# A hybrid decoder layer on one core: the middle stage rewritten as one schedule by weight chunk

## The chip, the core and the metric

One core of a Trainium2 chip runs the whole kernel. TensorE (PE) multiplies and writes to PSUM (eight banks of 512 columns), VectorE (DVE) and ScalarE (ACT) work between PSUM and SBUF, GpSimd (POOL) on SBUF alone, and SyncE (SP) issues most DMAs. Each engine runs its own instructions in order, and they wait for one another on semaphores. The metric is the device time of an execution in microseconds; lower is better.

## The reference

256 prompt tokens of one sequence and one new token for each of 8 decoding sequences (264 columns, N) go through one layer, in fp32:

```
x = LN(a*x + 0.5*(silu(x Wg) * (x Wu)) Wd)          # D 2048, F 5632
z = x W_in -> q, k, v (8 heads, 2 maps of 64) | b, c, h (1024 each) | gate_attn, gate_conv (2048 each)
q, k = rope(q), rope(k)
o = (softmax(q1 k1) - lam * softmax(q2 k2)) v        # prompt: causal over 256
                                                     # samples: 8 pages of 128 cached keys/values each, and the new token
y_attn = (headnorm(o) * g * 0.8) W_attn_out
y_conv = (b * conv3(c * h)) W_conv_out
x = LN(a*x + (sigmoid(gate_attn)*y_attn + sigmoid(gate_conv)*y_conv) W_o)
x = LN(a*x + 0.5*(silu(x Wg2) * (x Wu2)) Wd2)
```

Outputs are x, the new keys and values, and the last convolution inputs. `page_table` says which 128-row page of `cache_k` and `cache_v` each of a sequence's 8 pages is.

## The kernel before

**Chunks and products.** Activations lie with features on partitions and the 264 tokens in the free dimension. Every fp32 operand is split in a high and a low part that TensorE takes in a fast fp32 form (F32R), and a product of 128 x 128 weights is three matmuls (`products`, L512 to L514: x_hi w_hi, x_lo w_hi, x_hi w_lo). Weights come in chunks of 512 KB, 256 rows by 512 columns: SP loads one into a slot of `w_raw` (a ring of 4, `chunk`, L356), ACT copies it rounded to `w_hi` (`split_hi`, L845), DVE subtracts to get `w_lo` (`split_lo`, L1144), and PE runs 24 matmuls. The load of chunk n waits for the split of chunk n - 4, ACT's split waits for PE to have used chunk n - 4. ACT and DVE are written three chunks ahead of PE (LEAD). A panel is the sum over chunks for 512 output columns (four PSUM banks, one for each 128 columns): 8 chunks for `w_in`, 4 for the two inner projections. In most places two sets of four banks alternate.

**The stages.** First feed-forward block and norm; queries (two panels side by side, 16 chunks); keys (16); values (16); b, c, h (48 chunks, all on banks 0 to 3); three of four pairs of gate panels in a loop (48); two panels of the conv output (8); then the last gate pair (16) and the last two conv panels (8) with the value pages between their chunks; then the attention output, `W_o`, norm, second feed-forward block and norm.

**Keys of the samples.** The sample queries are stored to memory and broadcast to all partitions (`q_bcast`, all eight sequences, L482 and L485, on POOL's queue). A page of keys is loaded into one of two or four slots (`k_page`, L388), multiplied on POOL (L495), and summed by head on DVE (L1349). 16 pages go with the value panels, one page a chunk; the other 48 with every second chunk up to the last gate loop.

**Prompt attention.** It stands between the chunks of b, c, h, one head every five chunks (`at_head`): scores of both maps (L690, L691; map 0 on partitions 0 to 63, map 1 on 64 to 127; banks 4 and 5), mask and maximum on DVE, exp on ACT, weights on DVE (L1446, L1449), three transposes (L699), values (L708 to L710). The head norm squares two heads at a time on ACT, sums over partitions with a matmul of ones on 512 columns (L742, L812), takes roots and scales on DVE (L1474, L1476).

**Values of the samples.** A page goes through the weight ring: it is loaded into `w_raw`, split by ACT and DVE like a weight chunk, and multiplied by the page's weights, high and low in 16 columns (`page_values`, L783: four matmuls of 512 columns to 16 partitions). After 8 pages ACT copies the sums out and `turn_seq` turns them with one-column matmuls (L798), at every second sequence with the new token's values (L794). At the end come the samples' norm (L825) and the split of o into `o_hi` and `o_lo` (L1109, L1601), for which the first products of the attention output wait.

Of the kernel before, what the change touches and what calls it, by code (L numbers as in the profile page):

```python
# [8 lines left out]

# [6 lines left out]
ALU = mybir.AluOpType  # L16
ACT = mybir.ActivationFunctionType
F32 = mybir.dt.float32
# [4 lines left out]
P = 128  # L23
# [24 lines left out]
PT = 2  # L48

# [50 lines left out]
def program(nc, a, out):  # L100
    with ExitStack() as ctx:
# [38 lines left out]
        page_ids = at("page_ids", [1, B * PAGES], I32)  # L140
# [21 lines left out]
        o_all = at("o_all", [P, HEADS, N])  # L162
        scores = at("scores", [P, B, SLOTS, 2 * HEADS])
        k_ring = at("k_ring", [P, 2, DC])
        qb_at = (top + 31) // 32 * 32
        q_bcast = at("q_bcast", [P, B, DC])
        m_hi = at("m_hi", [P, DT, N], F32R, qb_at)
        m_lo = at("m_lo", [P, DT, N], F32R, qb_at + DT * TILE)
        v_s = at("v_s", [B, DC])
        assert 2 * DT * TILE <= (B + 1) * DC * 4  # L170
        early = (top + 31) // 32 * 32

        z_q = at("z_q", [P, AT, N])
        z_k = at("z_k", [P, AT, N])
        v_tok = at("v_tok", [P, PT, DC])
        z_v = at("z_v", [P, AT, N])

        zv_at = early + 2 * AT * TILE + PT * DC * 4
# [4 lines left out]
        top = early  # L183
        sig = at("sig", [P, 2, DT, N])
        assert zv_at + AT * TILE <= top

        c_at = top
# [3 lines left out]
        qk_tok = at("qk_tok", [P, 3, DC], F32, c_at + AT * TILE)  # L191

        k_slots = [k_ring[:, 0], k_ring[:, 1], qk_tok[:, 0], qk_tok[:, 1]]
        stats = at("stats", [P, 16])
        s_tmp = at("s_tmp", [B, 2, 2 * HEADS])

        u = z_c[:, 2]
        conv_o = z_c[:, 1]
        conv_t = at("conv_t", [P, 3, AT, B], F32, ln_at)
        conv_new = at("conv_new", [P, AT, B, 2], F32, ln_at + 768)  # L200
        o_sqp = at("o_sqp", [P, 2, T], F32, ln_at + 1280)
        yc_hi = at("yc_hi", [P, AT, N], F32R, c_at)
        yc_lo = at("yc_lo", [P, AT, N], F32R, c_at + 2 * AT * TILE)
        o_hi = at("o_hi", [P, AT, N], F32R, c_at)
        o_lo = at("o_lo", [P, AT, N], F32R, c_at + AT * TILE)

        kr_at = qb_at - 2 * DC * 4
        s_max = at("s_max", [P, P], F32, kr_at)
        s_diag = at("s_diag", [P, P], F32, kr_at + 512)
        s_rec = at("s_rec", [P, P], F32, kr_at + 1024)  # L210
        s_attn = at("s_attn", [P, B, SLOTS, HEADS], F32, kr_at + 1536)
        s_attn2 = at("s_attn2", [P, B, SLOTS, HEADS], F32, kr_at + 4096)
        s_col = at("s_col", [P, 1], F32, kr_at + 7168)

        s_weights = at("s_weights", [P, B, PAGES, 2, HEADS], F32R, qb_at)
        s_sums = at("s_sums", [2 * HEADS, DC], F32, qb_at + 4096)
        o_sqs = at("o_sqs", [P, HEADS * B], F32, qb_at + 8192 + 32)
        own_head = at("own_head", [2 * HEADS, HEADS], F32, qb_at + 8192)
# [41 lines left out]
        new_scored = sem("new_scored")  # L260
        q_stored = sem("q_stored")
        qb_landed = sem("qb_landed")
        k_landed = [sem(f"k_landed{i}") for i in range(4)]
        k_mult = sem("k_mult")
        k_free = sem("k_free")
        sc_done = sem("sc_done")
# [7 lines left out]
        o_ready = sem("o_ready")  # L274
        conv_done = sem("conv_done")
# [11 lines left out]
        ss_rec = sem("ss_rec")  # L287
        ss_attn = sem("ss_attn")
        pv_weights_hi = sem("pv_weights_hi")
        pv_weights = sem("pv_weights")  # L290
        seq_out = sem("seq_out")
        seq_turned = sem("seq_turned")
        seqs_out = sem("seqs_out")
        o_square = sem("o_square")
        o_normed = sem("o_normed")
        o_sumsq = sem("o_sumsq")
        o_std = sem("o_std")
# [18 lines left out]
        CONSTS, MADE = 16 * 7, 8  # L316
# [3 lines left out]
        V_TURN, K_BACK, FIRST_HEAD, HEAD_CH = 1, 5, 7, 5  # L320
# [6 lines left out]
        TURN_EVEN = {K_CH: 3, A_CH: 2}  # L327

        def through_page(chunks, k):

            c = next(c for c in range(chunks) if sum(PAGES_AFTER[chunks][:c + 1]) >= k)
            return c + 1 + k

        def sums_bank(b):

            return 4 * (1 - b // 2 % 2) + (2 if b % 2 == 0 else 0)

        HEAD_NORM = 3

        def at_head(h):  # L340
            return FIRST_HEAD + HEAD_CH * h

        assert at_head(HEADS) <= 2 * C_PAIRS * K_CH - 1
        assert KC * WC == DC and 2 * len(VALUE_PANELS) == B


        @block.sync
        def _(sp):
            n = Count()
            pages = Count()  # L350
# [30 lines left out]
            def page_numbers(seq):  # L381

                return nc.values_load_multi_w_load_instructions(
                    page_ids[0:1, bass.ds(seq * PAGES, PAGES)], engines=[mybir.EngineType.SP],
                    min_val=0, max_val=a["cache_k"].shape[1] - 1)[1]

            def page(cache, p, dst):
                return sp.dma_start(dst, cache[0, bass.ds(p, 1)].rearrange("a k h e -> (a k) (h e)"))  # L388

            def w_in_panel(i, p, after=None):  # L390
                for c in range(K_CH):
                    chunk(a["w_in"][0], KC * c, i * (2 * WC) + p * WC)
                    if after is not None:
                        after(c)

            def k_page(seq_ids, j, slot, free):
                sp.wait_ge(k_free, free)
                page(a["cache_k"], seq_ids[j], k_slots[slot]).then_inc(k_landed[slot], 16)

            def w_in_pair(i, seq):  # L400

                ids = page_numbers(seq)
                for p in range(2):
                    def keys(c):
                        if c % 2 == 1:
                            j = (p * K_CH + c) // 2
                            k_page(ids, j, j % 2, pages.add())
                    w_in_panel(i, p, keys)
# [5 lines left out]
            for p in range(2):  # L414
                w_in_panel(1, p)

            sp.wait_ge(page_ids_in, 16)
            sp.wait_ge(back, 1)
            seq_ids = []

            def keys(c):
                if c == 0:
                    return
                for j in (c - 1,) if c < 2 * K_CH - 1 else (c - 1, c):
                    if j % PAGES == 0:
                        seq_ids[:] = page_numbers(j // PAGES)
                    pages.add()
                    k_page(seq_ids, j % PAGES, j % 4, max(j - 1, 1))
            for p in range(2):
                w_in_panel(2, p, lambda c: keys(p * K_CH + c))  # L430
            with loop(sp, B - 2, (n, 2 * K_CH), (pages, PAGES)) as i:
                w_in_pair(i + 3, i + 2)

            def v_page(number):
                sp.wait_ge(w_lo_ready, n.add())
                s = (n.n - 1) % RING
                page(a["cache_v"], number, w_raw[:, s].rearrange("p k n -> p (k n)")).then_inc(w_landed[s], 16)

            out_pair(a["w_conv_out"][0], A_CH, 0)
            for p, chunks in enumerate(VALUE_PANELS):  # L440
                ids = []
                for c in range(chunks):
                    if chunks == K_CH:
                        chunk(a["w_in"][0], KC * c, (2 + C_PAIRS + G_PAIRS) * (2 * WC) + p * WC)
                    else:
                        chunk(a["w_conv_out"][0], KC * c, 2 * WC + (p - 2) * WC)
                    done = sum(PAGES_AFTER[chunks][:c])
                    for k in range(done, done + PAGES_AFTER[chunks][c]):
                        if k % PAGES == 0:
                            ids = page_numbers(2 * p + k // PAGES)  # L450
                        v_page(ids[k % PAGES])
# [13 lines left out]
        def _(pool):  # L465
# [5 lines left out]
            pool.wait_ge(made, 5)  # L471
# [5 lines left out]
            pool.dma_start(page_ids[:], a["page_table"]).then_inc(page_ids_in, 16)  # L477
# [5 lines left out]
            pool.wait_ge(q_stored, 16)  # L483
            for b in range(B):
                pool.dma_start(q_bcast[:, b], q_scratch[b:b + 1].broadcast_to([P, DC])).then_inc(qb_landed, 16)  # L485
            pool.wait_ge(qb_landed, 16 * B)

            for page in range(B * PAGES):
                if page < 2 * PAGES:
                    slot, uses = page % 4, page // 4 + 1  # L490
                else:
                    slot, uses = page % 2, 2 * PAGES // 4 + (page - 2 * PAGES) // 2 + 1
# [11 lines left out]
        def _(pe):  # L504
# [151 lines left out]
            for j in (2, 0, 1):  # L656
                to_tokens(z_q, j)
# [1015 lines left out]
```

## Time and profile before

| | |
|---|---|
| median of 3 runs | 2441.69 us (2439.89 to 2444.42) |
| profiled execution | 2443.84 us, span 2442.0 us |
| PE busy | 2363.0 us (97%), 18783 instructions |
| DVE busy | 1449.6 us (59%) |
| ACT busy | 1051.6 us (43%) |
| POOL busy | 192.6 us (8%) |
| HBM | 467.88 MB read, 193 GB/s over the span |

"Busy" of PE is a union of overlapping matmuls whose ends are modelled; the distance from one start to the next is what a matmul costs in a row of them. A row such as `L512 ... x2` in a timeline joins neighbouring records; a plain fp32 matmul has two records, a transpose or an F32R matmul one. The clock column is the granted share of 2.4 GHz, averaged over the stretch; in any moment it is 1.2 or 2.4 GHz.

### The profile page before, as it was taken

To read this page: it belongs to the slowest core of one execution; us is meant where nothing else is said; L and a number is where in the kernel's file an instruction comes from. 1 tells how busy PE (TensorE), PEld (TensorE's weight loads), DVE (VectorE), ACT (ScalarE), POOL (GpSimd) and SP (SyncE) were. 2 spreads that over 40 slices of the span, in tenths; PEclk is the share of its full clock that TensorE was granted. 3 is DMA by queue.
4 is the path that set the end of the run, shared out by engine and by line. 5 is a ranking of instruction groups with operands and counts; after the bars stand their busy time and mean duration, and the time that the engine had idled before them with its cause. 6 is when DMAs were issued, how large, how long until landed. Compare 5 with 4: busy or idle time off the path is not lost.

```text
span 2442.0 us, 46756 instructions
## 1 busy us (share of the span) xinstructions
PE 2363.0 (97%) x18783; PEld 2300.0 (94%) x18783; DVE 1449.6 (59%) x1494; ACT 1051.6 (43%) x1230; POOL 192.6 (8%) x98
## 2 busy tenths in 40 slices
PE   8999999999999999999899998999999999999997
PEld 8999999999998998888898767999999999999997
DVE  5444544545555768888887666777445444445554
ACT  4443444443333444444445554435444344444333
POOL 1000000000000036332340000000000000000001
PEclk9999999999999999999999998999999999999998
DMA  7655555555655587665676776555555555655553
GB/s 229 189 180 181 180 171 188 178 179 179 179 176 157 163 314 254 239 220 182 221 279 208 260 249 197 190 164 169 177 182 176 184 180 173 188 180 176 180 181 114
DMA packets 230518, 474.05 MB, mean 194 GB/s; under 512 B 16792, under 2 KB 18904, under 8 KB 230400
## 3 DMA queue, kind: packets, MB, share of 16 engines
q1 hardware_dynamic: 226304, 465.76, 59.4%
q0 software_dynamic: 1440, 4.38, 0.5%
q10 hardware_dynamic: 2656, 2.24, 0.3%
q8 instruction: 86, 1.41, 0.2%
q14 instruction: 32, 0.26, 0.0%
HBM read 467.88 MB, written 4.43 MB: 193 GB/s over the span
## 4 chain that ended last, share of the span: by engine, by line
PE 83%; DVE 9%; DMA 3%; ACT 3%; issue 2%; SPq 0%; DVEq 0%; ACTq 0%
PE ps L512 27%; PE ps L513 27%; PE ps L514 26%; DVE w_lo L1144 4%; DMA w_raw<-in_w_in 2%; ACT w_hi L845 1%; DVE scores L1349 1%; PE ps L783 1%; DMA w_raw<-in_cache_v 1%; PE ps L798 1%; DVE attn L1449 1%; DVE z_c L1500 0%; DVE o_sqp L1474 0%; DMA w_raw<-in_w_conv_out 0%; ACT prob L992 0%
## 5 line engine op out<-in xcount | busy, mean ns | idle before, releaser
L1144 DVE TENSOR_TENSOR w_lo<-w_raw,w_hi 128x1024 fp32r<-128x1024 f32 x816 | 1032.5, 1275 | 871.6 <-ACT w_hi L845 868.7
L845 ACT ACTIVATE w_hi<-w_raw 128x1024 fp32r<-128x1024 f32 x816 | 858.6, 1058 | 1087.4 <-PE ps L514 891.3
L512 PE MATMUL ps<-x_hi,w_hi 128*128 128x264 f32 x4096 | 1178.0, 288 | 37.8 <-DVE w_lo L1144 16.9
L513 PE MATMUL ps<-x_lo,w_hi 128*128 128x264 f32 x4096 | 1171.5, 286 | 0.0
L514 PE MATMUL ps<-x_hi,w_lo 128*128 128x264 f32 x4096 | 1170.5, 286 | 0.0
L512 PEld LDWEIGHTS ps<-x_hi,w_hi 128*128 128x128 f32 x4096 | 779.8, 190 | 51.0 <-DVE w_lo L1144 26.6
L513 PEld LDWEIGHTS ps<-x_lo,w_hi 128*128 128x128 f32 x4096 | 778.4, 190 | 1.0 <-issue 0.7
L514 PEld LDWEIGHTS ps<-x_hi,w_lo 128*128 128x128 f32 x4096 | 776.6, 190 | 0.0
L512 PE MATMUL ps<-h_hi,w_hi 128*128 128x264 f32 x1408 | 401.3, 285 | 0.0
L513 PE MATMUL ps<-h_lo,w_hi 128*128 128x264 f32 x1408 | 400.6, 285 | 0.0
L514 PE MATMUL ps<-h_hi,w_lo 128*128 128x264 f32 x1408 | 400.2, 284 | 0.0
L514 PEld LDWEIGHTS ps<-h_hi,w_lo 128*128 128x128 f32 x1408 | 265.3, 188 | 0.0
L513 PEld LDWEIGHTS ps<-h_lo,w_hi 128*128 128x128 f32 x1408 | 265.3, 188 | 0.1
L512 PEld LDWEIGHTS ps<-h_hi,w_hi 128*128 128x128 f32 x1408 | 264.5, 188 | 0.1
L495 POOL TENSOR_TENSOR k_ring<-k_ring,q_bcast 128x1024 f32<-128x1024 f32 x56 | 149.7, 2674 | 250.4 <-DMA k_ring<-in_cache_k 250.2
L499 POOL TENSOR_TENSOR y<-y,mean 128x528 f32<-128x528 f32 x5 | 6.3, 1300 | 1146.0 <-DVE mean L1281 1146.0
L512 PE MATMUL ps<-m_hi,w_hi 128*128 128x264 f32 x256 | 73.0, 285 | 0.0
L513 PE MATMUL ps<-m_lo,w_hi 128*128 128x264 f32 x256 | 72.8, 284 | 0.0
L514 PE MATMUL ps<-m_hi,w_lo 128*128 128x264 f32 x256 | 72.7, 284 | 0.0
L1349 DVE TENSOR_REDUCE scores<-k_ring 128x16 f32<-128x1024 f32 (+1 forms) x56 | 67.7, 1210 | 0.4
L482 POOL DMA_DIRECT2D q_scratch<-q_s x1 | 0.5, 531 | 841.5 <-DVE q_s L1394 841.5
L855 ACT ACTIVATE hid<-ps 128x264 f32<-128x264 f32 x88 | 34.2, 392 | 75.5 <-PE ps L514 75.5
(217 smaller groups left out, 1362.3 us busy)
## 6 DMA issues: line engine op xcount, KB each, us to landing
w_raw<-in_ffn_w_gate SPq DMA_DIRECT2D x176, 512.0 KB, 3.5
w_raw<-in_ffn_w_up SPq DMA_DIRECT2D x176, 512.0 KB, 4.3
w_raw<-in_ffn_w_down SPq DMA_DIRECT2D x176, 512.0 KB, 3.6
w_raw<-in_w_in SPq DMA_DIRECT2D x160, 512.0 KB, 5.0
w_raw<-in_cache_v SPq DMA_DIRECT2D x64, 512.0 KB, 4.5
k_ring<-in_cache_k SPq DMA_DIRECT2D x56, 512.0 KB, 3.9
w_raw<-in_w_o SPq DMA_DIRECT2D x32, 512.0 KB, 4.1
w_raw<-in_w_conv_out SPq DMA_DIRECT2D x16, 512.0 KB, 4.8
```

The source lines that it names most:

```text
L495: nc.gpsimd.tensor_tensor(keys, keys, q_bcast[:, page // PAGES], ALU.mult).then_inc(k_mult, 1)
L499: nc.gpsimd.tensor_tensor(two, two, mean[:].rearrange("p (a n) -> p a n", a=1).broadcast_to([P, KC, N]), ALU.subtract).then_inc(ln_centred, 1)
L512: nc.tensor.matmul(acc, wh, hi[:, kt], start=(kt == 0), stop=False)
L513: nc.tensor.matmul(acc, wh, lo[:, kt], start=False, stop=False)
L514: return nc.tensor.matmul(acc, wl, hi[:, kt], start=False, stop=last)
L783: mm = nc.tensor.matmul(ps[0:2 * HEADS, bank + c], s_weights[:, b, j].rearrange("p c h -> p (c h)"), w[:, s, c], start=(j == 0 and w is w_ ...
L798: mm = nc.tensor.matmul(by_head(b)[:, 0, h:h + 1], s_sums[:, h * VD:(h + 1) * VD], own_head[:, h:h + 1], start=False, stop=True, skip_grou ...
L845: nc.scalar.activation(w_hi[:, s], w_raw[:, s], ACT.Copy).then_inc(w_hi_ready, 1)
L855: nc.scalar.activation(dst(m), ps[:, 4 * banks + m, 0:N], func).then_inc(out_of[banks], 1)
L1144: V.tensor_tensor(w_lo[:, s], w_raw[:, s], w_hi[:, s].bitcast(F32), ALU.subtract).then_inc(w_lo_ready, 1)
L1349: V.tensor_reduce(dst, keys.rearrange("p (g d) -> p g d", d=HD), AX, ALU.add).then_inc(k_free, 1)
L1449: ins = V.scalar_tensor_tensor(attn[:, b].rearrange("p b k -> p (b k)"), prob[:, 1, b].rearrange("p b k -> p (b k)"), stats[:, 14 + j:15 + j],
```

## The change

Everything from the keys' panels to the last chunk before the attention output is written as one list of 160 chunks, x = 0 to 159, without loops. Each engine goes through the list, and constants say at which x each piece of other work stands (on DVE and ACT mostly x + 3 or more, because they run ahead).

- The order of panels: keys 2, values 2, b c h 6, conv gates 4, conv output 4, attention gates 4. All are summed in banks 0 to 3; banks 4 to 7 belong to the other work.
- One ring of nine page slots (`kv_ring`) holds key pages, then value pages. Key page j is summed at chunk 8 + 27 j // 25 (chunks 8 to 76). `q_bcast` holds four sequences; POOL issues the others' broadcasts between its multiplications.
- Value pages are no longer split. At 16 steps, every four chunks from 88 to 148, one page of each of four sequences is multiplied in plain fp32: 32 weight columns for each sequence, written to partitions 0, 32, 64 and 96, in two halves of 512 columns.
- The sums of four sequences are turned at once with the constant `pick`, the new token's share comes from DVE (`v_new`, `o_new`), and `v_sample` is stored transposed.
- Prompt attention: heads start at the chunks in HEAD; the values come with tokens on partitions, so that the head norm works per partition (square sums on ACT, root, scale), in groups of 3, 2 and 3 heads, which are turned back by transposes (`turn_out`). The weights are not scaled by the first map's sum before the product.
- The turns of q, k, v, the softmax of the samples, the convolution and the samples' norm are cut in pieces that stand at chunks of the list.

```diff
-        VALUE_PANELS = [K_CH, K_CH, A_CH, A_CH]
-        PAGES_AFTER = {K_CH: (3, 3, 2, 2, 2, 2, 2, 0), A_CH: (6, 5, 5, 0)}
+        for name, w, col, count, chunks in (
+                ("k", "w_in", DC, 2, K_CH), ("v", "w_in", 2 * DC, 2, K_CH), ("c", "w_in", 3 * DC, 6, K_CH),
+                ("conv_gate", "w_in", 6 * DC + D, 4, K_CH), ("conv_out", "w_conv_out", 0, 4, A_CH),
+                ("attn_gate", "w_in", 6 * DC, 4, K_CH)):
+            for i in range(count):
+                PANELS.append((name, i, w, col + i * WC, chunks))
+        Q_TURN, K_TURN, V_TURN, LAMBDA_SUM = 0, 2 * K_CH, 4 * K_CH, 8
+        K_SUM = [8 + 27 * j // 25 for j in range(B * PAGES)]
+        K_LOAD = [j - 2 * K_CH // 2 if j < PAGE_SLOTS else K_SUM[j] - 4 for j in range(B * PAGES)]
+        SOFTMAX = K_SUM[-1] + 1
+        NEW_TOKEN = SOFTMAX + 10
+        V_STEP = [SOFTMAX + 11 + 4 * s for s in range(2 * PAGES)]
+        V_LOAD = [K_SUM[B * PAGES - PAGE_SLOTS + v] + 5 if v < PAGE_SLOTS else V_STEP[v // SEQS] + v % SEQS - 1
+                  for v in range(B * PAGES)]
+        BY_HEAD = V_STEP[PAGES - 1] + 5, V_STEP[-1] + 3
+        HEAD = 40, 52, 64, 90, 100, 117, 127, 137
+        TURN, VALUES = 6, 8
+        NORMED = (0, 1, 2), (3, 4), (5, 6, 7)
+        CONV = 84
...
+            # PE
+            def page_values(step):
+                seqs, j = step // PAGES * SEQS, step % PAGES
+                for k in range(SEQS):
+                    i = B * PAGES + SEQS * step + k
+                    pe.wait_ge(kv_landed[i % PAGE_SLOTS], 16 * (i // PAGE_SLOTS + 1))
+                for half in range(2):
+                    for k in range(SEQS):
+                        at_page = ((seqs + k) * SLOTS + j) * HEADS
+                        rows = slice(k * P // SEQS, (k + 1) * P // SEQS)
+                        mm = nc.tensor.matmul(ps[rows, 6 + half], s_flat[:, at_page:at_page + P // SEQS],
+                                              kv_ring[:, (B * PAGES + SEQS * step + k) % PAGE_SLOTS,
+                                                      half * WC:(half + 1) * WC],
+                                              start=(j == 0), stop=(j == PAGES - 1), skip_group_check=True)
+                mm.then_inc(v_free, 1)
...
+            x = 0
+            for name, i, _, _, chunks in PANELS:
+                if name == "conv_out" and i == 0:
+                    pe.wait_ge(yc_ready, 2)
+                hi, lo = (yc_hi, yc_lo) if name == "conv_out" else (x_hi, x_lo)
+                for c in range(chunks):
+                    panel_chunk(0, hi, lo, c, chunks)
+                    middle(x)
+                    x += 1
...
+            # DVE
+            for x in range(LEAD, MIDDLE + LEAD):
                 split_lo(1)
+                if x - LEAD + 1 in ends:
+                    out_of_panel(*PANELS[ends.index(x - LEAD + 1)][:2])
+                for j in range(B * PAGES):
+                    if x == K_SUM[j]:
+                        page_scores(j)
+                for h in head_at(x, 4):
+                    prompt_max(h)
+                for h in head_at(x, 7):
+                    prompt_attn(h)
...
```

## Rows read from the trace of the kernel before

**Rows 1.** The page: its head, and from part 5 the split on DVE.
```profile
span 2442.0 us, 46756 instructions
...
L1144 DVE TENSOR_TENSOR w_lo<-w_raw,w_hi 128x1024 fp32r<-128x1024 f32 x816 | 1032.5, 1275 | 871.6 <-ACT w_hi L845 868.7
```

**Rows 2.** Table of stretches: from:to, length, busy time (instructions) by engine, clock, DMA.
```profile
core 0: us, PE busy (x) PEld busy (x) DVE busy (x) ACT busy (x) POOL busy (x), PEclk, DMA share, GB/s
300.00:400.00 100.00, 100.00 (x825) 100.00 (x824) 46.94 (x44) 41.36 (x45) 0.00 (x0) 1.00 0.58 180
790.20:839.80 49.60, 48.99 (x385) 48.84 (x386) 37.84 (x53) 25.06 (x38) 0.00 (x0) 0.95 0.55 170
839.80:1498.70 658.90, 614.59 (x4546) 554.67 (x4546) 509.48 (x510) 319.75 (x425) 180.06 (x73) 0.97 0.70 240
891.00:943.00 52.00, 49.94 (x389) 47.59 (x387) 51.93 (x33) 19.12 (x25) 43.95 (x14) 1.00 0.74 265
...
1498.70:1548.20 49.50, 49.50 (x385) 49.50 (x386) 32.55 (x39) 18.31 (x20) 0.00 (x0) 0.94 0.47 145
```

**Rows 3.** Timeline of PE (start us, us, records xN): one head; the queries' transposes.
```profile
839.78 2.78 PE L636 MATMUL ps<-ident,z_q 128*8 128x128 f32 x24 [0.57 <-ACT z_q L855]
...
1035.37 0.38 PE L708 MATMUL ps<-attn_t,v_tok 128*128 128x128 f32 x2
...
1036.13 0.50 PE L690 MATMUL ps<-z_k,z_q 64*128 64x128 f32 x4
1036.46 0.61 PE L691 MATMUL ps<-z_k,z_q 64*128 64x256 f32 x4
1036.99 0.39 PE L512 MATMUL ps<-x_hi,w_hi 128*128 128x264 f32 x1
```

**Rows 4.** Timeline of PE: turning a sequence's sums; value pages at both clocks.
```profile
1333.47 1.94 PE L794 MATMUL ps<-s_attn,v_s 8*128 8x2 f32 x16
1335.28 1.92 PE L798 MATMUL ps<-own_head,s_sums 16*128 16x1 f32 x16
...
1443.24 1.06 PE L783 MATMUL ps<-w_lo,s_weights 128*16 128x512 f32 x2
1444.10 1.06 PE L783 MATMUL ps<-w_hi,s_weights 128*16 128x512 f32 x2
...
1447.12 0.63 PE L783 MATMUL ps<-w_hi,s_weights 128*16 128x512 f32 x2
1447.59 0.62 PE L783 MATMUL ps<-w_lo,s_weights 128*16 128x512 f32 x2
```

**Rows 5.** Timeline of PE: a plain fp32 matmul of 512 columns.
```profile
1138.35 1.02 PE L742 MATMUL ps<-o_sqp,ones 128*128 128x512 f32 x2
...
1139.33 0.28 PE L513 MATMUL ps<-x_lo,w_hi 128*128 128x264 f32 x1
```

**Rows 6.** Waits of PE, 839.8 to 1498.7: total us, times, longest us.
```profile
PE ps L512 <- DVE w_lo L1144: 20.2, 23, 4.0
PE ps L699 <- DVE attn L1449: 9.0, 8, 3.5
...
PE ps L512 <- DVE o_lo L1601: 3.0, 1, 3.0
```

**Rows 7.** Timeline of DVE and POOL: key pages, at one a chunk and alone.
```profile
910.24 2.29 DVE L1144 TENSOR_TENSOR w_lo<-w_raw,w_hi 128x1024 fp32r<-128x1024 f32 x1
...
914.75 6.72 POOL L495 TENSOR_TENSOR k_ring<-k_ring,q_bcast 128x1024 f32<-128x1024 f32 x2
...
1252.51 2.40 POOL L495 TENSOR_TENSOR k_ring<-k_ring,q_bcast 128x1024 f32<-128x1024 f32 x1 [2.64 <-DMA k_ring<-in_cache_k]
```

**Rows 8.** POOL's timeline and line L485: broadcast of the sample queries, and its landing.
```profile
850.79 4.22 POOL L485 DMA_DIRECT2D q_bcast<-q_scratch  x8 [1.87 <-DMA q_scratch<-q_s]
...
DMA to landing us min/median/max: 6.6/11.5/18.1
```

**Rows 9.** The chain that ended last, 960 to 985: start us, us, what.
```profile
974.77 8.77 DMA w_raw<-in_w_in
```

More of the change, by code:

```diff
@@ L390, in w_in_panel, with page @@
[L390 to L408, printed above, removed]
+            def page(cache, number, i):
+                slot = i % PAGE_SLOTS
+                sp.dma_start(kv_ring[:, slot], cache[0, bass.ds(number, 1)].rearrange("a k h e -> (a k) (h e)")
+                             ).then_inc(kv_landed[slot], 16)
@@ L413, in _ @@
                     chunk(a["w_in"][0], KC * c, p * WC)
[L414 to L441, printed above, removed]
-                for c in range(chunks):
[L443 to L451, printed above, removed]
+                    pages(2 * (c - K_CH) + p)
+            x = 0
+            for _, _, w, col, chunks in PANELS:
+                for c in range(chunks):
+                    chunk(a[w][0], KC * c, col)
+                    pages(x)
+                    x += 1
             out_proj(a["w_attn_out"][0], A_CH)
@@ L776, in page_values @@
-            def page_values(b, j):
-                pe.wait_ge(w_lo_ready, n.add() + RING)
-                s = (n.n - 1) % RING
-                bank = sums_bank(b)
-                for w in (w_hi, w_lo):
-                    for c in range(KC):
-                        mm = nc.tensor.matmul(ps[0:2 * HEADS, bank + c], s_weights[:, b, j].rearrange("p c h -> p (c h)"),
-                                              w[:, s, c], start=(j == 0 and w is w_hi), stop=(j == PAGES - 1 and w is w_lo))
-                mm.then_inc(w_used, 1)
@@ L1352, in _, with page_scores @@
[L1352 to L1371 removed]
+            def page_scores(j):
+                keys = kv_ring[:, j % PAGE_SLOTS]
+                v.wait_ge(k_mult, j + 1)
+                V.tensor_reduce(scores[:, j // PAGES, j % PAGES], keys.rearrange("p (g d) -> p g d", d=HD),
+                                AX, ALU.add).then_inc(k_free, 1)
@@ L1515, in _ @@
-            with loop(v, G_PAIRS - 2, *at_.steps(K_CH), (k_turn, PAGES), (own, 2)) as i:
-                page = page_scores(i + (3 + C_PAIRS))
-                split_lo(HEAD_NORM + 2, page)
-                head_norm(i + 1, page)
-                split_lo(2 * K_CH - (HEAD_NORM + 2) - 2, page)
-                at_.skip_panel(0, K_CH)
-                at_.skip_panel(1, K_CH)
-            def gate_tile(c, t):
-                return sig[:, c, bass.ds(t, 1)].rearrange("p a n -> p (a n)")
-            for banks in range(2):
-                v.wait_ge(out_of[banks], out_n[banks]())
@@ new lines, in out_of_panel @@
+            def out_of_panel(name, i):
+                if name != "conv_out":
+                    at_.skip_panel(0, K_CH)
+                    return
+                for m in range(MC):
+                    wait_tile(m, A_CH)
+                    g = sig_conv[:, MC * i + m]
+                    V.tensor_tensor(g, g, ps[:, m, 0:N], ALU.mult).then_inc(out_of[0], 1)
+                    out_n[0].add()
+            ends = list(itertools.accumulate(chunks for *_, chunks in PANELS))
+            assert n.n == CHUNKS_BEFORE + LEAD, n.n - CHUNKS_BEFORE
```

990 lines of the change are left out of this document (479 added, 511 removed).

## The prediction

> **What bounds the kernel now.** I read the page first [rows 1]: the profiled execution took 2443.84 us around a span of 2442.0, and the median of the runs shown is 2441.69, so the sum below is made on the trace and its difference taken off 2441.69. Then the table of stretches [rows 2]. In a stretch of the first feed-forward block PE starts 825 matmuls in 100 us, 0.1213 us each, and is never idle: this is the pace of the 264-column product, 24 to a weight chunk, 2.91 us a chunk. The stretch that the change rewrites runs from the turn of the queries (839.8) to the first product of the attention output (1498.7): 658.9 us, in which PE has 160 chunks of the same products, 3840 x 0.1213 = 466 us. The other 193 us are small PE work and waits; the clock is 0.97 in the mean, and DVE is busy 509 of the 659 us, so only PE is near full.
>
> The timelines price the small work. One head's values take 1035.37 to 1036.13, 0.76 us, its scores 0.86 us to 1036.99, and a transpose at most 2.78/24 = 0.116 us [rows 3]. One value page costs two pairs of 16-column matmuls 0.47 us apart, 0.94 us [rows 4]: 64 pages, 60 us. Turning a sequence's sums costs 1.81 us, and every second one 1.81 more [rows 4]: 12 x 1.81 = 22 us. With 129 transposes (15), eight heads (13), four squared sums over the heads at 0.86 (3) [rows 5] and 5 us for starting the products again after small work this is 466 + 60 + 22 + 15 + 13 + 3 + 5 = 584. The rest, 75 us, is waiting and lowered clock. The waits of PE name 20 us for w_lo, 9 for the heads' weights, 3 for o_lo [rows 6], the longer ones; in the page stage there are stretches at 1.2 GHz, where two 512-column matmuls stand 0.86 us apart (1443.24 to 1444.10) against 0.47 at 2.4 GHz [rows 4].
>
> **The change part by part.**
> Unchanged on PE: 160 chunks, 466 us, plus 5 for restarts.
> Removed: 64 pages through the weight ring (60 us of PE, and 64 splits on ACT and DVE; DVE's cost 1.28 each in the mean [rows 1]), 12 turns of sums (22), four squared sums (3).
> Added: 16 page steps. Each is eight plain fp32 matmuls with 32 weight columns, over 512 columns, in four column groups, two halves one after the other. The trace has no column groups. Bounds: a plain 512-column matmul alone takes 0.86 us (1138.35 to 1139.33 is 0.98 and holds one product of 0.12) [rows 5]. All eight in series are 6.9 us; four side by side 1.72. I take side by side, because the trace has the like across rows of the array: the scores of a head's two maps lie on partitions 0 to 63 and 64 to 127, the program orders L690, L691 of map one and then of map two, and the timeline shows four L690 records together and then four L691 [rows 3]. 768 columns at 0.86/512 would be 1.29 us in series, 0.65 side by side; 0.86 was taken. So overlap is real and costs 0.2 us around it: a step is 1.92, 16 steps are 31 us (series: 7.1, 114 us).
> By-head sums: 2 x 8 small plain matmuls, priced as the turn: 3.6. Transposes: 24 + 24 + 16 of q, k, v, 32 back, 24 in heads, 16 of outputs, 1: 137 x 0.116 = 16. Heads' scores and values: 8 x 1.62 = 13. Four small matmuls against ones: 1.
> Without waits PE has 466 + 5 + 31 + 3.6 + 16 + 13 + 1 = 535.6 us.
>
> The waits. *Key stage.* One key page now goes with every 1.08 chunks, from DVE's chunk 8 to 76. That pace exists in the trace: from 891 to 943 each chunk had a page, POOL took 6.72 us for two multiplications (3.36 each, against 2.40 alone), and w_lo took 2.29 us while POOL worked [rows 7]. So POOL's multiplication and the split exclude each other: a page takes 2.40, and a split 0.95 of POOL's time. 64 pages with 69 splits are 154 + 66 = 220 us, and 10 more for rope, the new token, three heads and four query broadcasts. The first can start when a broadcast query has landed, 6.6 us at least after issue at 850.8 [rows 8], some 3 us later here (the query goes out after chunk 1): 860. The stage ends at 1090. PE by itself would be through chunk 76 at 839.8 + 77 x 2.91 + 96 transposes (11) + three heads (5.8) + restarts (2) = 1083. That is 7 us lost. Weights that land late add 10: with pages and the 1 MB stores of k and v under way a weight chunk took 8.77 us [rows 9], and a ring of four chunks has about 11.6 less 2.4 of splits. I take 17, between nothing (nine page slots decouple POOL) and 60 (every split waits a whole multiplication).
> *The new wait at DVE's chunk 8* for the first product of keys has behind it DVE's own splits; PE has three chunks in hand, 8.7 us, against 3 to 5 of lateness: nothing, and if it is later, us for us.
> *Pages on SP.* They wait for slots freed at least one chunk earlier; behind them on SP stand weight loads, and behind PE's wait for a page's landing all its products. A page is asked for 8 chunks before POOL's product is summed and, for values, some 3 chunks before its step, 9 us against 4 to 6 of landing: nothing. The table of stretches shows 265 GB/s carried in 891 to 943; here it is 1 MB in 3.3 to 3.5 us, 300 to 315. While the first nine pages load, beside the query panels (16 chunks in 49.6 us [rows 2]), it is 340: 1 us lost.
> *Panels on four banks.* The taking out of tile m must end before PE is back at m, 2.2 us later; it takes 0.4 us. It does so on ACT or, for the conv output, on DVE. Nothing, unless those are late; then each of 24 panels can pay 1 us.
> *Softmax, conv, norms, by-head sums* stand in chunk slots one to three chunks before PE asks. The largest slot is four conv instructions, under 3 us. I give all of these, with late values, 8 us (0 to 30).
> *The end.* The samples' norm was in the open (PE waited for o_sqs and 3 us for o_lo, and the clock fell, 0.94 in the next stretch, which took 49.5 us [rows 2, 6]). Now it lies beside the last chunks. That stretch has 384 products, 46.6 us: 2.6 gained on average, between 0 and 2.9.
>
> The sum: 535.6 + 17 + 8 = 560.6 against 658.9 is 98.3 less; 2.6 less after it, 1 more before it: 100 us. 2441.7 - 100 = **2342 us**.
>
> **A rule against it.** The rows show records of two row groups out of program order [rows 3]. The Trainium skill (TensorE: Matmul & The Clock Gate, Part 3, Packing small matmuls) says that matmuls in different tiles start and end strictly in program order. By that, only the second pass of one matmul could lie beside the first of the next; the sum would be 2375 us, and it stands below as a rival, priced from rows.
>
> **The rivals.**
> *Page steps overlap in pairs only.* 16 passes of 0.43 in 9 slots, 4.0 us a step, 33 more in all: 2375. For it: all four groups read the same 128 rows, which the scores did not. 10 in 100.
> *Page steps in series.* 16 x 7.1 = 114, 83 more, less some 5 of other waits that it would cover: 2420. For it: no column group is in the trace. Against: the row groups did overlap, and across records of other instructions [rows 3]. 13.
> *The key stage becomes DVE's.* Each head's DVE work and rope stand behind splits that wait for POOL; at 3.9 us a chunk instead of 3.3 over 69 chunks it costs 40 more: 2382. For it: DVE and POOL have no slack there. Against: the nine slots. 9.
> *The waits only move.* The 75 us of before return as late landings, four-bank hand-overs and softmax steps: 50 more than I give, 2392. That the change does not do what it says is part of this. 6.
> *Slower.* The page steps run in series and the clock stays at 1.2 GHz through them, as where 16-column matmuls ran for long [rows 4]: 16 x 7.1 x 2 = 227 us, 196 more, 2538. It decides against the change from 8.2 us a step. Against: four chunks of full products lie between steps, and in the stretch without waits the clock was 1.00 [rows 2]. 4.
>
> **The numbers.** The forecast holds 58 in 100 with a range of its own of 2315 to 2372. With no wait at all it would be 2317; 2308 and below needs PE's own work cheaper than I price it (a transpose at less, a page step at 1.7). The range 2308 to 2420 takes in pairs, key stage, moved waits and most of the series case; out are the slow rival, half of series and what is below. This kernel's measurement can tell 0.2%, 5 us. All but the slow case and a little of the moved waits are faster: faster 0.93, same 0.02, slower 0.05.
>
> **What would show it.** In the changed profile the stretch from the last query product to the first product of the attention output should be 550 to 575 us. A page step should stand 1.9 us before the next product with four starts within 0.1 us; 4.0 or 7.1 says which rival. POOL should be busy nearly without a gap for some 220 us, with w_lo at 2.2 us, and PE's waits for w_lo should lie there. No wait for o_lo should stand before the attention output, and the clock should be 1.00 after the key stage. The feed-forward stretches should keep 825 matmuls in 100 us; if they don't, the forecast is wrong where I didn't look.

## The result, and the profile after

The changed kernel takes 2353.58 us (median of 4 runs, 2352.49 to 2356.22) against 2442.32 for the kernel before; the ratio is 0.9639, 95% interval 0.9622 to 0.9655. It is 88.7 us faster. The forecast was 2342 us, 100 less than before, and the range 2308 to 2420. The profiled execution took 2352.54 us around a span of 2350.7, 91.3 us less than the span of the trace on which the forecast was worked out.

The table of stretches of the changed kernel, same columns as [rows 2]: the stretch, PE, PEld, DVE, ACT and POOL busy with the instructions started, the granted clock, DMA share and GB/s.

```profile
300.00:400.00 100.00, 100.00 (x825) 100.00 (x824) 46.93 (x44) 41.28 (x45) 0.00 (x0) 1.00 0.54 180
790.60:840.10 49.50, 49.50 (x390) 49.50 (x391) 37.79 (x53) 25.08 (x39) 0.00 (x0) 0.95 0.76 266
840.10:1410.20 570.10, 541.65 (x4384) 509.67 (x4382) 415.48 (x398) 261.38 (x395) 192.75 (x73) 0.98 0.79 269
840.10:1118.10 278.00, 249.59 (x1996) 245.69 (x1994) 263.74 (x200) 117.57 (x173) 192.75 (x73) 0.95 0.82 288
1118.10:1410.20 292.10, 292.05 (x2392) 263.98 (x2390) 151.74 (x199) 143.82 (x222) 0.00 (x0) 1.00 0.76 251
1410.20:1457.20 47.00, 47.00 (x385) 46.98 (x385) 31.71 (x37) 19.05 (x22) 0.00 (x0) 1.00 0.49 161
```

The rewritten stretch, 658.9 us before [rows 2], takes 570.1. It has two halves. From the end of the keys on (1118.1) PE is idle for 0.05 us in 292 and the clock is 1.00: there PE runs without waits. In the key stage, 840.1 to 1118.1, PE is idle for 28 us, the clock is 0.95, and DVE is busy for 264 of 278 us. So the time that was lost is in the key stage. PE's waits in the whole stretch (total us, times, longest us), to be held against [rows 6]:

```profile
PE ps L643 <- DVE qk_tok L1310: 17.0, 1, 17.0
PE ps L674 <- DVE attn L1353: 7.4, 3, 3.3
PE ps L512 <- ACT z_c L820: 2.6, 1, 2.6
PE ps L512 <- DVE w_lo L1094: 1.0, 2, 0.8
PE ps L512 <- ACT z_k L820: 0.4, 1, 0.4
```

The first is one wait that the forecast did not have: PE wants to turn the roped keys back (`from_tokens`, chunk 21), and the rope on DVE isn't done. The timeline of DVE, POOL and PE there (start, us, instruction, idle time before it and who ended it):

```profile
907.81 2.47 DVE L1305 TENSOR_TENSOR rope_t<-qk_tok,rope_cs 8x128 f32<-8x128 f32 x1
910.21 0.27 DVE L1306 TENSOR_TENSOR rope_t<-qk_tok,rope_cs 8x128 f32<-8x128 f32 x1
...
910.43 0.59 POOL L481 DMA_DIRECT2D q_bcast<-q_scratch  x1 [0.30 <-POOL kv_ring L495]
910.61 12.12 DVE L1308 TENSOR_TENSOR rope_t<-qk_tok,rope_cs 8x128 f32<-8x128 f32 x1
911.04 11.55 POOL L495 TENSOR_TENSOR kv_ring<-kv_ring,q_bcast 128x1024 f32<-128x1024 f32 x5
...
928.50 0.42 DVE L1310 TENSOR_TENSOR qk_tok<-rope_t 128x256 f32<-128x256 f32 x1
...
929.06 1.30 PE L643 MATMUL ps<-ident,qk_tok 128*128 128x128 f32 x5 [17.02 <-DVE qk_tok L1310]
```

A multiplication of 8 x 128 elements, 0.27 us otherwise, takes 12.12 us, just as long as POOL multiplies five key pages without a break. Below, such an instruction is called held. And by group from 860 to 1118 (busy us, mean ns, idle before):

```profile
L1094 DVE TENSOR_TENSOR w_lo<-w_raw,w_hi 128x1024 fp32r<-128x1024 f32 x71 | 142.9, 2017 | 2.5 <-ACT w_hi L810 2.5
...
L495 POOL TENSOR_TENSOR kv_ring<-kv_ring,q_bcast 128x1024 f32<-128x1024 f32 x64 | 187.7, 2955 | 46.1 <-DMA kv_ring<-in_cache_k 42.9 <-DMA q_bcast<-q_scratch 3.2
```

POOL, which was to be the busy one, stands idle for 43 us for want of pages. SP asks for each page behind a weight load, and what SP waits for in the key stage is DVE's splits alone (the weight loads of L372, 68 times, 186.7 us); no wait for a page slot is in its view. So a late DVE makes the pages late too: behind the held instruction POOL waits 7.06 us for the next page.

A page step (start, us from its first start to its last end):

```profile
1154.43 0.28 PE L514 MATMUL ps<-x_hi,w_lo 128*128 128x264 f32 x1
1154.64 1.92 PE L704 MATMUL ps<-kv_ring,s_flat 128*32 128x512 f32 x16
1156.49 0.39 PE L512 MATMUL ps<-x_hi,w_hi 128*128 128x264 f32 x1
```

1.85 us from its first start to the next product, 1.92 forecast: sixteen records of 0.6 us, in four sets 0.43 to 0.45 us apart, the four of a set within 0.02 us.

### The profile page after: what moved, and what is told of

It is laid out like the page before. It is cut to its first block, busy times and chain, and to the rows that moved or that the text cites. A ratio compares the mean times of both kernels' runs of the same rounds, so it can differ in the third digit from the quotient of the medians.

```text
span 2350.7 us, 45699 instructions
## 1 busy us (share of the span) xinstructions
PE 2287.9 (97%) x18625; PEld 2253.0 (96%) x18625; DVE 1354.5 (58%) x1381; ACT 995.1 (42%) x1204; POOL 206.0 (9%) x101
## 4 chain that ended last, share of the span: by engine, by line
PE 87%; DVE 10%; DMA 1%; issue 1%; ACT 1%; POOL 0%; ACTq 0%; SPq 0%; DVEq 0%
PE ps L512 29%; PE ps L513 28%; PE ps L514 28%; DVE w_lo L1094 5%; DVE scores L1294 3%; PE ps L704 1%; DVE rope_t L1308 1%; DMA w_raw<-in_w_in 0%; ACT y_norm L898 0%; PE ps L608 0%; ACT w_hi L810 0%; DMA q_bcast<-q_scratch 0%; DVE attn L1353 0%; DMA w_raw<-in_ffn_w_gate 0%; DVE stats L1341 0%
## 5 line engine op out<-in xcount | busy, mean ns | idle before, releaser
L1094 DVE TENSOR_TENSOR w_lo<-w_raw,w_hi 128x1024 fp32r<-128x1024 f32 x752 | 971.9, 1299 | 890.4 <-ACT w_hi L810 888.3
L810 ACT ACTIVATE w_hi<-w_raw 128x1024 fp32r<-128x1024 f32 x752 | 792.2, 1059 | 1084.4 <-PE ps L514 1031.3
L495 POOL TENSOR_TENSOR kv_ring<-kv_ring,q_bcast 128x1024 f32<-128x1024 f32 x64 | 187.7, 2955 | 46.1 <-DMA kv_ring<-in_cache_k 42.9
L1294 DVE TENSOR_REDUCE scores<-kv_ring 128x16 f32<-128x1024 f32 x64 | 77.3, 1208 | 2.6 <-POOL kv_ring L495 2.5
```

The source lines that it names most:

```text
L495: nc.gpsimd.tensor_tensor(keys, keys, q_bcast[:, b % SEQS], ALU.mult).then_inc(k_mult, 1)
L810: nc.scalar.activation(w_hi[:, s], w_raw[:, s], ACT.Copy).then_inc(w_hi_ready, 1)
L1094: V.tensor_tensor(w_lo[:, s], w_raw[:, s], w_hi[:, s].bitcast(F32), ALU.subtract).then_inc(w_lo_ready, 1)
L1294: V.tensor_reduce(scores[:, j // PAGES, j % PAGES], keys.rearrange("p (g d) -> p g d", d=HD), AX, ALU.add).then_inc(k_free, 1)
```

## The experiments

All are edits of the changed kernel; "before" ran beside each on the same chip. Each expectation was written before its run.

**Rope of the new tokens out of the way.**

```diff
-  if x == K_TURN + 5:   # DVE: rope(B, PT, PT + 1), the 8-row rope of k
+  if x == K_TURN + 11:  # ...and new_scores from K_TURN + 13 on (was + 9)
```

> The rope of the new tokens' keys (six instructions on 8 partitions) moves from DVE's chunk 21 to chunk 27, behind the rope of the prompt's keys (chunk 23); what hangs on it moves 4 chunks later. Theory A: in the changed kernel PE's longest wait, 17.0 us for the prompt's rope, is mostly one 8-partition instruction (L1308) that DVE could not finish for 12.1 us while POOL multiplied five pages back to back; with the small instructions behind it, PE waits only for DVE's usual lateness, about 4 us, so the kernel takes 2353.6 - 13 = 2341 us (2337 to 2345), the products after the turn of k start near 917 instead of 929. A second hold may come at chunk 27, but there PE has three chunks of weights in hand. Rival B: POOL and DVE together bound the whole key stage (64 x 2.4 + 69 x 0.95 = 219 us of exclusive time, plus heads), so that what is won at chunk 23 is lost again before the last key page: no more than 3 us faster, 2350 to 2354, key stage still ending near 1118.

Measured: 2356.73 us, ratio 0.9644 [0.9625, 0.9663]: no gain. No instruction is held, and the wait is as long (timeline):

```profile
909.67 18.08 POOL L495 TENSOR_TENSOR kv_ring<-kv_ring,q_bcast 128x1024 f32<-128x1024 f32 x7
...
913.08 2.55 DVE L1307 TENSOR_TENSOR rope_t<-qk_tok,rope_cs 128x256 f32<-128x256 f32 x1
915.56 2.56 DVE L1308 TENSOR_TENSOR rope_t<-qk_tok,rope_cs 128x256 f32<-128x256 f32 x1
...
928.17 2.15 PE L643 MATMUL ps<-ident,qk_tok 128*128 128x128 f32 x9 [17.50 <-DVE qk_tok L1312]
```

The six instructions of the other rope, 0.42 us each when POOL is idle, now take 2.55: one multiplication of POOL before each. My theory A fell: the held instruction is one form of the cost; six turns in a row are another, at the same price, as long as POOL has pages in hand. B was nearer for the time (its range ended at 2354), not for its reason (it spoke of a bound over the whole stage).

**No multiplication of keys.**

```diff
-  nc.gpsimd.tensor_tensor(keys, keys, q_bcast[:, b % SEQS], ALU.mult)
+  nc.gpsimd.tensor_tensor(keys[:, 0:8], keys[:, 0:8], q_bcast[:, b % SEQS, 0:8], ALU.mult)
```

> Leaves out most of the multiplication of the key pages: POOL multiplies 8 of 1024 columns (the scores of the pages are wrong by that). Loads, sums and order are unchanged. Theory A and B alike (POOL's multiplications and DVE's splits exclude each other): w_lo falls from 2.3 to 1.22 us, the 17.0 us wait is gone, PE runs the key stage at its own pace and passes chunk 76 at 1083 to 1090 instead of 1118: 2353.6 - 31 = 2322 us (2318 to 2327). Rival C: the key stage is late because 300 GB/s of weights and pages land late: then the same 3.5 to 4 us stay lost between two heads and the time is 2337 or more, only the 17 us wait gone.

Measured: 2315.35 us, 0.9474 [0.9456, 0.9492], 38.2 below the changed kernel. The stretch until chunk 76 is passed, and w_lo from 860 on in it:

```profile
840.00:1081.50 241.50, 241.50 (x1997) 239.56 (x1995) 187.95 (x200) 118.14 (x174) 28.75 (x73) 1.00 0.93 333
...
L1094 DVE TENSOR_TENSOR w_lo<-w_raw,w_hi 128x1024 fp32r<-128x1024 f32 x71 | 86.8, 1224 | 44.0 <-ACT w_hi L810 43.6
```

PE is never idle, though the queues carry 333 GB/s against 288 in the changed kernel's key stage. So rival C falls: neither late weights nor pages cost anything. All 36.6 us that the key stage loses (1118.1 against 1081.5) come from POOL's multiplications. The time is 7 us below the 2322 expected and just outside the range given: they cost more than either theory had.

**Page steps in one column group; and in another order.**

```diff
-  rows = slice(k * P // SEQS, (k + 1) * P // SEQS)
+  rows = slice(0, P // SEQS)   # start and stop once for the four sequences of a half
```

```diff
-  for half in range(2):
-      for k in range(SEQS):
+  for k in range(SEQS):
+      for half in range(2):
```

> The four sequences of a page step all use columns 0 to 31 of the array and partitions 0 to 31 of the banks (their values are added up, and the rest of the banks keeps old data, so the attention over pages is wrong). Same matmuls, same bytes, same waits. Theory: the 1.85 us of a step rest on four column groups that run side by side. In one group eight matmuls of 0.86 us stand one behind the other: 6.9 to 7.1 us a step, 16 x 5.15 = 82 us more, 2436 us (2428 to 2440; less where value pages that land late would have been waited for). Rival: the overlap is in the records only and PE is limited by something else: no difference, 2354.

> In a page step the loops change places: both halves of a sequence, then the next sequence, so that two matmuls of one column group follow each other. Nothing else changes. Theory O (a matmul waits only for those of its own columns, whatever the order): 1.85 us a step, 2353.6 (2352 to 2356). Rival P (starts strictly in program order, as a rule of the Trainium skill has it: TensorE: Matmul & The Clock Gate, Part 3, Packing small matmuls): four passes of 0.43 us for each sequence, of which only the last can lie beside the first of the next group: 16 - 3 = 13 slots of 0.43, 5.6 us a step, 16 x 3.7 = 60 us more, 2413 us (2400 to 2420).

Measured: 2437.8 us, 0.9973 [0.9954, 0.9991], for one group; 2354.86, 0.9632 [0.9613, 0.9652], for the other order. Timelines of PE, first with one group:

```profile
1158.22 7.05 PE L704 MATMUL ps<-kv_ring,s_flat 128*32 128x512 f32 x16
1165.20 0.40 PE L512 MATMUL ps<-x_hi,w_hi 128*128 128x264 f32 x1
```

then by sequence:

```profile
1158.75 1.94 PE L704 MATMUL ps<-kv_ring,s_flat 128*32 128x512 f32 x16
1160.63 0.39 PE L512 MATMUL ps<-x_hi,w_hi 128*128 128x264 f32 x1
```

In one group a step is 6.98 us, as the bound of eight matmuls in series said; 16 x 5.13 = 82 us, and 84 came. Without the column groups the whole change would have been worth 0.3%, about 5 us between the medians. With the order turned a step stays at 1.88 us. Its sixteen records again start in four sets of four, 13 ns apart within a set and 0.43 to 0.45 us from set to set. In the kernel with one group records stand 0.43 to 0.45 us apart, so the four starts of a set can't be those of matmuls of one group: a later matmul in another group starts ahead of an earlier one. The rule of the Trainium skill that was weighed in the prediction (TensorE: Matmul & The Clock Gate, Part 3, Packing small matmuls) would by the expectation's working have given 5.6 us. Here the measurement decides against it.

**Less for POOL, more for DVE.**

```diff
+  if j % 4 == 3: V.tensor_tensor(keys, keys, q_bcast[:, b % SEQS], ALU.mult)   # on DVE; POOL skips it
-  pool.wait_ge(k_mult, PAGES * b)   # POOL, ahead of the broadcast of query b + 3
+  pool.wait_ge(k_free, PAGES * b)   # ...which so waits until DVE has summed the pages
```

> DVE itself multiplies every fourth key page (1.13 us by the w_lo of the same size) and POOL the other three. Theory S (POOL's multiplications and DVE's two-input instructions take one resource in turns, and that resource bounds the key stage): four chunks take 4 x 0.95 + 3 x 2.40 + 1.13 = 12.1 us of it, 3.04 a chunk instead of 3.35; with the heads the stage ends near 1100 instead of 1118: 2353.6 - 16 = 2338 us (2330 to 2344). The wait for the rope of k stays for the most part (POOL has four multiplications in hand instead of five: 12 to 17 us). Rival D (DVE's own work is the bound): 16 multiplications more on DVE are 18 us more, 2354 to 2372.

Measured: 2374.96 us, 0.9718 [0.9702, 0.9734], 21 slower than the changed kernel: theory S gave the wrong sign, and the time is over rival D's range too. The timeline shows something that neither theory had:

```profile
888.25 1.22 DVE L1097 TENSOR_TENSOR w_lo<-w_raw,w_hi 128x1024 fp32r<-128x1024 f32 x1
888.87 0.59 POOL L482 DMA_DIRECT2D q_bcast<-q_scratch  x1 [11.18 <-DVE scores L1303]
889.48 13.98 POOL L498 TENSOR_TENSOR kv_ring<-kv_ring,q_bcast 128x1024 f32<-128x1024 f32 x6
...
893.06 11.49 DVE L1097 TENSOR_TENSOR w_lo<-w_raw,w_hi 128x1024 fp32r<-128x1024 f32 x1
...
904.60 0.59 PE L515 MATMUL ps<-x_hi,w_hi 128*128 128x264 f32 x1 [8.60 <-DVE w_lo L1097]
```

A split is held until POOL has no page left, and there are four such places in this kernel (11.5, 15.2, 11.5, 11.5 us), each behind a DMA that POOL issued:

```profile
PE ps L515 <- DVE w_lo L1097: 34.0, 5, 9.6
```

The second line of the edit counts as well: before each of the four issues POOL now stands 11 to 24 us waiting for DVE's sums, and goes on with a store of pages in hand. So the run doesn't price the moved multiplications alone.

**A gap in the pages round the rope of k; and with DVE's fourth.**

```diff
-  K_SUM = [8 + 27 * j // 25 ...]; K_LOAD: K_SUM[j] - 4
+  K_SUM = [8 + j if j < 13 else 13 + j ...]; K_LOAD: K_SUM[j] - 1 to - 3 from the 14th page on
```

> The key pages are spaced anew: 13 pages at DVE's chunks 8 to 20, none at 21 to 25, one a chunk from 26 to 76; and from the 14th page on they are asked for one to three chunks ahead instead of four, so that POOL has nothing in hand when DVE ropes k (chunks 21 and 23). Theory S: the 17 us of PE's wait are small two-input instructions of DVE, each of which waits for POOL; without pages in hand the wait is 0 to 2 us, and from there 51 chunks with a page take 3.35 us each and 9 for three heads: chunk 76 is passed near 1098 instead of 1118: 2353.6 - 20 = 2334 us (2328 to 2342). Rival B (it only moves: POOL needs the pauses' time later): 2350 or more.

> Both edits: the gap round the rope of k and every fourth multiplication on DVE. Theory S: no wait for the rope, 3.04 us a chunk against PE's 2.91 and its small work: the stage ends within 4 to 9 us of the 1081 that it reaches without any multiplication: 2353.6 - 30 = 2323 us (2318 to 2330). Theory D (DVE's own work bounds): no better than the gap alone, 2334 or more.

Measured: 2348.28 us, 0.9606 [0.9585, 0.9627], and 2361.23, 0.9662 [0.9646, 0.9679]. With the gap PE's wait for the rope is gone, but the waits for attention and w_lo are 21.7 us in place of 8.4, so 13 of the 17 us come back (waits of PE with the gap alone):

```profile
PE ps L674 <- DVE attn L1353: 14.0, 3, 6.2
PE ps L512 <- DVE w_lo L1094: 7.7, 7, 3.0
```

The rival that it only moves is nearer than theory S: 5 us gained of 20. The kernel with both was expected at 2323 by theory S and is 38 us slower than that; it has four held instructions again (6.9, 9.2, 4.6, 10.7), and POOL's wait for DVE's sums before each issue.

**Multiplications in halves.**

```diff
+  for part in (slice(0, WC), slice(WC, DC)):
+      mul = nc.gpsimd.tensor_tensor(keys[:, part], keys[:, part], q_bcast[:, b % SEQS, part], ALU.mult)
```

> POOL multiplies each key page in two instructions of 512 columns instead of one of 1024. Theory T (they take turns instruction by instruction: a waiting instruction of DVE gets in after the one that POOL is at): the rope's small instructions and each split wait half as long, w_lo 1.6 to 1.8 us instead of 2.3, the wait for the rope of k 8 to 10 us instead of 17, 2353.6 - 8 = 2345 us (2340 to 2349), less what 64 more instructions cost on POOL. Theory U (POOL keeps the resource until it runs out of pages in hand, as the 12.1 us instruction beside five multiplications 2.30 us apart suggests): the wait stays 15 us or more, 2351 to 2358.

Measured: 2344.61 us, 0.9596 [0.958, 0.9612], as theory T has it, and the wait for the rope is 6.5. The mean of w_lo is 1.71 us, which seems to be T's number but counts one of 18.0; the others have 1.5. For here too one instruction is held, and by this one U is true:

```profile
886.80 0.59 POOL L481 DMA_DIRECT2D q_bcast<-q_scratch  x1 [0.30 <-POOL kv_ring L496]
887.41 17.21 POOL L496 TENSOR_TENSOR kv_ring<-kv_ring,q_bcast 128x512 f32<-128x512 f32 x14
887.67 18.03 DVE L1096 TENSOR_TENSOR w_lo<-w_raw,w_hi 128x1024 fp32r<-128x1024 f32 x1
...
905.76 0.59 PE L514 MATMUL ps<-x_hi,w_hi 128*128 128x264 f32 x1 [15.05 <-DVE w_lo L1096]
```

So there are two regimes: mostly turns, instruction by instruction; after some DMA issues of POOL, none.

**No DMA on POOL between multiplications.** ACT issues the broadcasts of queries 4 to 7, in three kernels: with halves, with DVE's fourth, with halves and the gap.

```diff
-  pool.wait_ge(k_mult, PAGES * b); query(b + SEQS - 1)       # POOL
+  sc.wait_ge(k_free, PAGES * b)                              # ACT, 3 chunks after K_SUM[8 b - 1]
+  sc.dma_start(q_bcast[:, s % SEQS], q_scratch[s:s + 1].broadcast_to([P, DC])).then_inc(qb_late[b - 1], 16)
```

> As the kernel with half multiplications (2344.6 us), and the broadcasts of queries 4 to 7 are issued by ACT instead of POOL, so that POOL issues no DMA between multiplications. All ten instructions of DVE that were held for 4.6 to 18 us in the runs so far (one in the changed kernel, four each in two others, one with halves) began within 6 us of such an issue on POOL, and none elsewhere. Theory H (after a DMA issue POOL doesn't give the shared resource back before it runs out of pages): no DVE instruction over 4 us in the key stage; the 18.0 us w_lo and PE's wait of 15.1 us for it are gone: 2344.6 - 14 = 2331 us (2327 to 2336). Rival R (the holds come from the backlog of pages and fall beside the issues by chance): a hold of over 8 us stays, 2341 or more.

> As the kernel in which DVE multiplies every fourth page (2375.0 us), and queries 4 to 7 are issued by ACT. Theory H: its four holds (11.5, 15.2, 11.5, 11.5 us) go, and with them PE's 34 us of waits for w_lo: 2375 - 34 = 2341 us (2336 to 2348). Theory D (DVE's 16 multiplications more are what cost): 2365 or more, though the holds go.

> Queries by ACT, half multiplications and the gap of pages round the rope of k. Theory H and S: on top of 2331 the 6.5 us wait for the rope of k goes, but the 51 pages after the gap come one a chunk, 3.35 us of POOL and split against 2.91 of PE: 4 to 6 of the 6.5 are lost again: 2329 us (2322 to 2335). Rival (the tighter pages cost more than the rope's wait): over 2335.

Measured: 2339.76 us, 0.9583 [0.9566, 0.96]; 2354.44, 0.9653 [0.9632, 0.9673]; 2339.27, 0.9582 [0.9563, 0.9601]. Theory H holds in all three: no DVE instruction of the key stage is longer than 2.4 us with halves or 3.4 with whole multiplications. With DVE's fourth this gives 20.5 us back (34 expected; 2354.44 lies between the ranges of H and D), and the kernel is where the changed kernel was: moving every fourth multiplication is worth nothing. The 20.5 can't be put down to the holds alone, as POOL's waits for DVE's sums went with them. With halves it gives 4.9 (14 expected): PE's 15.1 us at the split are gone, but its wait for the rope grows from 6.5 to 17.0, since the rope's instructions now all take turns, 1.2 to 1.5 us each (PE's waits, halves):

```profile
PE ps L643 <- DVE qk_tok L1317: 17.0, 1, 17.0
PE ps L674 <- DVE attn L1360: 4.5, 3, 2.4
```

With the gap on top that wait is 2.6 us, and 11.2 stand before the heads' attention; DVE itself now waits 43.9 us for products that POOL has not made yet. Nothing gained, the rival's reason.

**PE asks for the rope later.**

```diff
-  if x == K_TURN + 5:   # PE: from_tokens() of k (ACT takes it out 4 chunks later too)
+  if x == K_TURN + 9:
-  if x == K_TURN + 5:   # DVE: 8-row rope, as in the first experiment
+  if x == K_TURN + 11:
```

> As the kernel with half multiplications and queries 4 to 7 by ACT (2339.8 us, in which PE still waits 17.0 us for the rope of k: twelve small instructions of DVE, each 1.3 to 1.5 us long because each waits for half a multiplication of POOL). Here PE asks for the roped k four chunks later (25 instead of 21; the first head needs it at 40), and the rope of the new tokens moves from DVE's chunk 21 to 27, what hangs on it 4 chunks later. Theory Q (PE waited only because it asked too early; DVE's lateness of 8.4 us for six instructions fits within the three chunks, 8.7 us, that PE has in hand): the wait is 0 to 3 us, 2339.8 - 14 = 2326 us (2321 to 2331), chunk 76 is passed near 1089. Rival W (DVE's delay only comes out at another place, as waits for w_lo or for the heads): no more than 5 us gained, 2335 or more.

Measured: 2337.5 us, 0.9557 [0.9529, 0.9584]: no difference from 2339.8 that can be told. Rival W is right. The wait for the rope is gone, and PE loses the time at w_lo instead (PE's waits, then the stretch of the two ropes):

```profile
PE ps L512 <- DVE w_lo L1103: 11.8, 5, 5.3
...
901.50:962.70 61.20, 49.44 (x355) 48.38 (x354) 59.80 (x46) 19.86 (x24) 61.20 (x36) 0.89 0.75 258
```

POOL is busy for 61.2 of 61.2 us and DVE for 59.8. Together they are the bound there, whatever PE asks for first. This is the lowest time of the kernels that do all the work, 16 us under the changed kernel (the intervals 0.9529 to 0.9584 and 0.9622 to 0.9655 are apart) and 4.4% under the kernel before; most of that came with the halves.

## Why the prediction was right, point by point

The stretch was forecast at 535.6 + 17 + 8 = 560.6 us and took 570.1: 533.6 of PE's own work, 36.6 lost in the key stage and nothing behind it.

*PE's own work, 535.6 us.* Right: 241.5 in the key stage without multiplications plus 292.1 after it are 533.6. The pace of the product was kept, 825 in 100 us as in [rows 2], and a page step is 1.85 us against 1.92; the two L690, L691 records of [rows 3] were enough to see that parts of the array work side by side, and the experiment with one group shows that 82 us hung on it.

*The key stage, 17 us lost.* This is the term that was mis-sized: 36.6. The working took POOL's 2.40 and the split's 0.95 as exclusive [rows 7] and laid one page beside one split; that is right (3.35 us a pair in the changed profile). It then put "10 more for rope, the new token, three heads" and spread all over nine page slots. The runs show that DVE's small instructions are not small beside POOL: one of 0.27 to 0.42 us waits for a multiplication of 2.4. Two ropes are twelve of them, and a head has four that are drawn out (1.47, 1.02 and two in 2.79 us in the first head, 0.17, 0.22 and 0.75 without the multiplications). Of the 36.6 us, 17.0 are the rope's wait, here mostly one held instruction of 12.1, 1.4 the transposes behind it (16 in 3.02 us at a mean clock of 0.55, against 1.66 for the roped queries), and 7.4 are waits for the heads' attention. Of the other 11, 4.4 lie in the 192 products from 965.94 (27.91 us, 23.5 without the multiplications; 2.6 of them are the wait for ACT's z_c), and 3 behind the waits for the first two heads, where the clock had fallen: 48 products in 7.44 us at a mean clock of 0.78, 5.91 without the multiplications. So at least 4 us of the loss are at the lower clock that follows PE's waits, a term that the sum did not have. The 10 us for late weights were wrong in kind: without multiplications nothing is late at 333 GB/s. Two of the signs asked for failed with this term: POOL was idle for 46 us where it was to be busy nearly without a gap, and PE waited 1.0 us for w_lo, its waits being those for the rope and the heads. Nine slots don't help DVE either: they give POOL pages in hand, and DVE takes turns with them or is held through them.

*The new wait at DVE's chunk 8, pages on SP, four banks.* Nearly right: DVE waited 2.5 us once, PE for no page, and PE waited 2.6 us once for ACT's taking out, where the sum had nothing; that wait is gone without the multiplications.

*Softmax, conv, norms, late values, 8 us.* Too much: PE is idle for 0.05 us after 1118.1. 8 too many here and 2 in PE's own work make up for half of the 20 too few in the key stage; that much of the forecast's nearness is luck.

*The end.* Right: the attention output takes 47.0 us, 49.5 before [rows 2], with no wait for o_lo and the clock at 1.00. The query stage lost nothing, where 1 us was given: 49.5 us, 49.6 before [rows 2].

*The rivals.* Pairs and series are out by the step's 1.85 us. "The key stage becomes DVE's" named the mechanism, rope and heads behind splits that wait for POOL, at 40 us; it came to half of that and is in the forecast's mis-sized term. I held the nine slots against it, and that was the error.

## What to carry to other kernels

Where two engines take turns, count instructions, not busy time: each of DVE's costs it up to a whole instruction of the other one, so keep POOL's short (9 us gained here) and DVE's few. To keep POOL short of work while DVE has a chain of small steps took PE's wait for the chain away, but gained 5 us with whole multiplications and none with halves. Before a cost is blamed on a wait, take away what is suspected to cause it (here 8 columns instead of 1024), for moving the wait gained nothing three times and 5 of 17 us once. Column groups of the array are worth looking for where a stationary operand is 32 columns wide: here they brought a step from 6.98 to 1.85 us.

## What the runs showed of the hardware

*Turns.* A two-input DVE instruction beside POOL's two-input multiplications waits for the one under way: w_lo takes 1.22 us alone and mostly 2.3 beside whole multiplications; beside half ones most take 1.2 and some 2.3, 1.5 in the mean. The sums of pages (tensor_reduce) never wait (1.20 to 1.22 in all). A tensor_scalar of 128 x 4 with one input was drawn out too (0.17 alone, up to 2.08). The Trainium skill (SBUF — State Buffer, Who interferes with whom) has this as an exclusive lock for the whole of an instruction. The turns agree with it; the held instructions, which wait through several of POOL's, go beyond it.

*Held instructions.* In eight kernels POOL issued 32 DMAs between multiplications; behind 12 of them, 0.2 to 4.2 us later, a DVE instruction began that did not end before POOL had run out of pages, through up to 14 multiplications 1.22 us apart. In four kernels without such issues there was none. That is what the profiled executions show; what decides between the 12 and the 20 stays open. Two things stand out in the traces, neither tried by itself. In the two kernels whose POOL waits for DVE's sums before it issues, all 8 issues had a hold; in the other six 4 of 24. And in 19 of the 20 without a hold a two-input instruction of DVE that had begun before the issue ran 0.1 to 0.2 us beyond its end (883.75 in the changed kernel); in none of the 12 did one run more than 0.01 us beyond it.

*Order.* Matmuls in different column groups lie beside each other even where the program puts two of the same group in a row: 1.88 us for a step of eight in that order, 1.85 in the other, 6.98 in one group.
